# Input projection and attention of the first block merged into one loop of 32 steps, the adaptive sums moved into two down projections

## What is computed

```
proj = h @ w_in                      # q (16 heads x 64), k and v of 3 branches (4 groups x 64), gates
k_cmp, v_cmp, k_sel, v_sel, k_win, v_win = ...
kc = gelu(blocks(k_cmp + pos) @ w1[0]) @ w2[0]      # 31 blocks of 32 tokens, stride 16
vc = gelu(blocks(v_cmp + pos) @ w1[1]) @ w2[1]
o_cmp = softmax(q . kc, masked) @ vc                # 31 keys
o_sel = softmax(q . k_sel, causal) @ v_sel          # up to 512 keys
o_win = softmax(q . k_win, causal) @ v_win          # up to 512 keys
o = gate0 * o_cmp + gate1 * o_sel + gate2 * o_win
return o @ w_out
```

## Time and profile before

| | us |
|---|---|
| median of 3 runs | 2434.73 (2434.29 to 2435.03) |
| the profiled execution's own time | 2437.86 |
| its span | 2436.1 |
| TensorE busy | 2296.4 (94%) |
| DVE / ACT / POOL busy | 1389.7 / 822.6 / 254.3 |
| first matmul | 10.55 |
| last matmul of NSA_IN begins | 131.96 |
| first score of the attention | 160.49 |
| first matmul of NSA_OUT | 481.29 |

### The profile page before, as it was taken

The page is one execution under the profiler, slowest core; times in us unless marked ns, Lnnn a source line. Parts: engine busy times, 40 slices in busy tenths (PEclk is TensorE's granted clock), DMA queues, the critical chain, the costliest instruction groups (busy, mean ns, idle before and its releaser), DMA issues.

```text
span 2436.1 us, 28016 instructions
## 1 busy us (share of the span) xinstructions
PE 2296.4 (94%) x10752; PEld 1847.9 (76%) x10752; DVE 1389.7 (57%) x2557; ACT 822.6 (34%) x1459; POOL 254.3 (10%) x199
## 2 busy tenths in 40 slices
PE   8988989989999998999868989999999998999997
PEld 6866667777888886888757868888877887888886
DVE  4367788657777336864777458776334645333323
ACT  4223344435443224443323334443222223222221
POOL 0035454320000002000241020000000000000000
PEclk9977889999999998999888999999988997999998
DMA  4442222123332331333000313333322221333331
GB/s 164 132 141 73 83 79 79 40 61 95 95 95 91 91 96 56 109 95 92 22 1 1 95 52 113 91 92 90 94 75 78 93 91 35 108 89 95 89 94 59
DMA packets 58804, 202.59 MB, mean 83 GB/s; under 512 B 6704, under 2 KB 6704, under 8 KB 58288
## 3 DMA queue, kind: packets, MB, share of 16 engines
q1 hardware_dynamic: 55920, 191.36, 25.9%
q10 hardware_dynamic: 2752, 9.44, 1.1%
HBM read 197.63 MB, written 2.10 MB: 82 GB/s over the span
## 4 chain that ended last, share of the span: by engine, by line
PE 87%; DVE 6%; issue 3%; POOL 2%; ACT 2%; DMA 0%; POOLq 0%; DVEq 0%; SPq 0%; ACTq 0%
PE bank L545 23%; PE bank L546 23%; PE bank L547 23%; PE bank L678 3%; PE bank L648 2%; PE bank L503 2%; PE bank L663 2%; PE bank L649 1%; POOL h L442 1%; PE bank L681 1%; PE bank L617 1%; PE bank L772 1%; PE bank L530 1%; DVE ssum L1232 1%; PE bank L806 1%
## 5 line engine op out<-in xcount | busy, mean ns | idle before, releaser
L545 PE MATMUL bank<-xhi,whi 128*128 128x512 f32 x1776 | 710.8, 400 | 28.0 <-DVE xlo L1212 22.6
L546 PE MATMUL bank<-xlo,whi 128*128 128x512 f32 x1776 | 708.4, 399 | 0.0
L547 PE MATMUL bank<-xhi,wlo 128*128 128x512 f32 x1776 | 707.8, 399 | 0.0
L1200 DVE TENSOR_TENSOR wlo<-raw,whi 128x1024 fp32r<-128x1024 f32 (+1 forms) x322 | 387.6, 1204 | 423.6 <-ACT whi L891 423.6
L891 ACT ACTIVATE whi<-raw 128x1024 fp32r<-128x1024 f32 (+1 forms) x322 | 334.8, 1041 | 808.1 <-PE bank L547 794.0
L545 PEld LDWEIGHTS bank<-xhi,whi 128*128 128x128 f32 x1776 | 337.5, 190 | 112.1 <-DVE xlo L1212 12.8
L547 PEld LDWEIGHTS bank<-xhi,wlo 128*128 128x128 f32 x1776 | 337.3, 190 | 82.5
L546 PEld LDWEIGHTS bank<-xlo,whi 128*128 128x128 f32 x1776 | 337.6, 190 | 81.8
L545 PE MATMUL bank<-hid_hi,whi 128*128 128x512 f32 x528 | 208.9, 396 | 0.0
L546 PE MATMUL bank<-hid_lo,whi 128*128 128x512 f32 x528 | 208.6, 395 | 0.0
L547 PE MATMUL bank<-hid_hi,wlo 128*128 128x512 f32 x528 | 208.6, 395 | 0.0
(11 more groups left out here) (265 smaller groups left out, 2756.8 us busy)
## 6 DMA issues: line engine op xcount, KB each, us to landing
raw<-w SPq DMA_DIRECT2D x298, 512.0 KB, 3.6
ada_w<-w_ada SPq DMA_DIRECT2D x64, 384.0 KB, 3.1
raw<-w SPq DMA_DIRECT2D x24, 384.0 KB, 3.1
h<-xT ACTq DMA_DIRECT2D x8, 256.0 KB, 9.3
w1st<-w_cmp ACTq DMA_DIRECT2D x1, 2048.0 KB, 14.3
w_v<-w_cmp ACTq DMA_DIRECT2D x1, 2048.0 KB, 8.3
out_t<-h ACTq DMA_DIRECT2D x8, 256.0 KB, 2.0
swp<-qkv ACTq DMA_DIRECT2D x2, 512.0 KB, 6.0
```

The costliest lines, as they stand in the source:

```text
L545: pe.matmul(bk, whi[w][:, cols], hi[:, k, :], start=first, stop=False)
L546: pe.matmul(bk, whi[w][:, cols], lo[:, k, :], start=False, stop=False)
L547: return pe.matmul(bk, wlo[w][:, cols], hi[:, k, :], start=False, stop=last)
L1200: dve.tensor_tensor(wlo[g % SLOTS][:, 0:n], raw[g % RAWS][:, 0:n], whi[g % SLOTS][:, 0:n].bitcast(F32), ALU.subtract).then_inc(s_lo, 1)
```

## The change

1. NSA_IN is put in another order: compressed k, compressed v, the four value panels, the gates, the first key panels, then q. Panels 13 to 20 are no longer multiplied ahead of the attention: they stand inside its loop as `filler`, two blocks (6 matmuls) a step, and panels 13 and 14 whole in two steps ahead of it.
2. Compression reads 33 columns per group with a stride of 16 out of a doubled copy (`dk`, `dv`: half of the partitions shifted by one token, made by four DMAs each, L1186). The position term is the 33rd column and comes in as the gelu's bias. `swp` and `flatten` are gone. `w1` is loaded at the start.
3. The attention has 32 steps s = (tile t, query panel qt), qt in the order 3, 2, 0, 1. A step holds four units (two branches r, two halves a). The compressed branch runs once per tile for all four query panels (`compressed_scores`, `compressed_masked`, `compressed_exps`, `compressed_scaled`, `turn_compressed`). All copies of transposed probabilities are ACT's. In `scores` and `pv` the two halves a alternate from one matmul to the next.
4. The first 6 of 8 blocks of the first three NSA_OUT panels stand in the last two steps (`out_ahead`).
5. The adaptive sums go out of the attention: 32 blocks into DOWN1 and 32 into DOWN2 (ring of 3, two accumulators). Their loads stand in SP's list two behind each of 16 weight panels; `spread_ada` stands ahead of tiles 3, 5, 6 and 7.

In the diff the three loops over i are those of TensorE, ACT and DVE, in this order; behind them stand the loads in SP's list and the line in `gemm`.

```diff
+STEPS = 32
+QT_ORDER = (3, 2, 0, 1)
...
+FILLER = {-2: [(13, kb) for kb in range(8)], -1: [(14, kb) for kb in range(8)]}
+for _m in range(6):
+    for _r in range(4):
+        FILLER[4 * _m + _r] = [(15 + _m, 2 * _r), (15 + _m, 2 * _r + 1)]
...
+            def compress_in(kv):
...
+                        mm = pe.matmul(bank[kv][:, hh * 132:(hh + 1) * 132], w1[:, m, hh * P:(hh + 1) * P],
+                                       dup[:, :, 2 * m:2 * m + 16 * 32 + 1:16], start=m == 0, stop=m == 15)
...
+            def scores(s):
...
+                for r in range(2):
+                    for a in range(2):
+                        rows, g = slice(a * HD, (a + 1) * HD), 2 * r + a
+                        if s:
+                            pe.wait_ge(s_sc, 4 * (s - 1) + g + 1)
+                        pe.matmul(bank[g][:, 0:n], qb[rows, t, qt * P:(qt + 1) * P], kb_[rows, r, j, 0:n],
+                                  start=True, stop=True).then_inc(s_S, 1)
...
+            def pv(s):
...
                 for r in range(2):
                     for kb in range(qt + 1):
+                        for a in range(2):
+                            g = 2 * j + a
+                            pe.matmul(out_slice(qt)[a * HD:(a + 1) * HD, :],
+                                      vtok[:, kb, r * 256 + g * HD:r * 256 + (g + 1) * HD],
+                                      pt[:, s % 2, 2 * r + a, kb * P:(kb + 1) * P], start=r == 0 and kb == 0,
+                                      stop=False, skip_group_check=True)
...
+            for i in range(-2, STEPS + 1):
...
+                if i + 2 < STEPS:
+                    scores(i + 2)
+                units = turned_units(i) if 0 <= i < STEPS else []
+                for u in range((len(units) + 1) // 2):
+                    turn(i, u)
+                filler(i)
+                if i >= STEPS - 1:
+                    for kb in range(3):
+                        out_ahead(3 * (i - STEPS + 1) + kb)
+                for u in range((len(units) + 1) // 2, len(units)):
+                    turn(i, u)
+                if units and i % 4 == 0:
+                    turn_compressed(i // 4)
+                if i >= 0 and after_step(i) is not None:
+                    compressed_scores(after_step(i))
+                if i >= 1:
+                    pv(i - 1)
...
+            for i in range(-2, STEPS + 2):
+                if i - 1 in PANEL_ENDS:
+                    weight_hi(PANEL_ENDS[i - 1] + SLOTS)
...
+                if i >= 2:
+                    out_hi(i - 2)
+                if 0 <= i < STEPS:
+                    keep_turned(i)
+                if i + 2 < STEPS:
+                    exps(i + 2)
+                if i >= 0 and after_step(i) is not None:
+                    compressed_exps(after_step(i))
...
+            for i in range(-2, STEPS + 2):
+                if i - 1 in PANEL_ENDS:
+                    nsa_take(PANEL_ENDS[i - 1], 7)
...
+                if i >= -1 and i + 1 < STEPS:
+                    scaled(i + 1)
+                if i >= 2:
+                    out_low(i - 2)
+                if i + 2 < STEPS:
+                    masked(i + 2)
+                if i >= 0 and after_step(i) is not None:
+                    compressed_masked(after_step(i))
...
+                if i - 1 in PANEL_ENDS:
+                    weight_lo(PANEL_ENDS[i - 1] + SLOTS)
+                if i % 4 == 2 and (i + 2) // 4 < 8:
+                    compressed_scaled((i + 2) // 4)
...
+                for half, name in enumerate(("DOWN1", "DOWN2")):
+                    k = g - START[name] - 7
+                    if 0 <= k < 16:
+                        sp.wait_ge(s_pe, START[name])
+                        for n in (2 * k, 2 * k + 1):
+                            load_ada(KD * ADA_HALF * half + n)
...
+                    if ada is not None and t in ADA_TILES:
+                        spread_ada(ada + ADA_TILES.index(t))
```

More of the change, by code:

```diff
@@ L556, in gemm @@
                     for kb in range(nb):
+                        if off + kb < skip or (only is not None and off + kb >= only):
+                            continue
                         pe.wait_ge(s_xt, XT[name] + off + kb + 1)
@@ L565, in gemm @@
                                 mm.then_inc(s_pe, 1)
+                if only is not None:
+                    return
                 if q is not None:
@@ new lines, in _ @@
+            whole(K_FIRST, 3)
+            pe.wait_ge(s_gelu, 2)
+            pe.wait_ge(s_v, 1)
+            for g in range(4):
+                for hh in range(2):
+                    mm = pe.matmul(bank[4][(g % 2) * HD:(g % 2 + 1) * HD, (g // 2) * NC:(g // 2 + 1) * NC],
+                                   w2[0][:, hh, :], hg[:, hh, g, 0:NC], start=hh == 0, stop=hh == 1)
+            mm.then_inc(s_cm, 1)
+            pe.wait_ge(s_ev, taken(GATES))
+            whole(K_FIRST + 1, 2)
+            pe.wait_ge(s_gelu, 4)
@@ new lines, in compressed_scores @@
+            def compressed_scores(t):
+                pe.wait_ge(s_ev, taken(Q_PANEL[t]))
+                for a in range(2):
+                    turn_bank_free(pe, SCORE_AT[t] + a)
+                for qt in range(NT):
+                    for a in range(2):
+                        rows = slice(a * HD, (a + 1) * HD)
+                        mm = pe.matmul(turn_bank(SCORE_AT[t] + a)[:, 32 * qt:32 * qt + NC],
+                                       qb[rows, t, qt * P:(qt + 1) * P], kct[rows, t // 4, :], start=True, stop=True)
+                mm.then_inc(s_cs, 1)
@@ L684, in spread_ada @@
-            def spread_ada(t):
-                pe.wait_ge(s_ada_k, KD + KD * t)
-                for f in range(ADA_SLICE // P):
-                    mm = pe.matmul(bank[2][:, 256 + f:257 + f], ada_acc[:, f * P:(f + 1) * P], ones[:, 0:1],
-                                   start=True, stop=True)
-                mm.then_inc(s_adap, 1)
-            def tile(t, j, jp):
-                for k in range(8 if j is not None else 4):
-                    for stage, lag in ((scores, 0), (pv, 4), (turn, 2)):
-                        at_ = unit(k, lag, t, j, jp)
-                        if at_:
-                            stage(*at_)
@@ new lines, in pv, with filler @@
+                for a in range(2):
+                    mm = pe.matmul(out_slice(qt)[a * HD:(a + 1) * HD, :], vz[:, qt, 2 * j + a, :],
+                                   ptc[:, t % 2, a, :], start=False, stop=True, skip_group_check=True)
+                mm.then_inc(s_pv, 1)
+            def filler(i):
+                for c, kb in FILLER.get(i, ()):
+                    if kb == 0:
+                        pe.wait_ge(s_lo, c + 1)
+                        pe.wait_ge(s_ev, taken(c - 1))
+                    mm = product(psum_ap(7), c, kb, kb, kb == KD - 1, xhi, xlo)
+                    if kb == KD - 1:
+                        mm.then_inc(s_pe, 1)
```

745 lines of the change are left out of this document (425 added, 320 removed).

## The result

| | us |
|---|---|
| before, median of 4 runs | 2434.88 (2434.29 to 2436.27) |
| changed kernel, median of 4 runs | 2326.11 (2324.71 to 2331.31) |
| ratio | 0.9543, 95% interval 0.9515 to 0.9572 |
| profiled execution of the changed kernel; its span | 2324.71; 2323.0 |

The change saves 108.8 us. The forecast was 2304 us, 22 less than measured and inside its range.

A forecast was written before the change was run, and what follows sets the result against it. Stages were taken as bounded by TensorE, the new attention loop by the DVE and ACT chain. -151.4 us through the attention and +20.6 in DOWN1 and DOWN2 give -130.8 on 2434.7: 2304 us, range 2272 to 2350.

The forecast's parts named there:

- Ahead of the loop: Before the attention loop: eight panels moved out, compression products 7.9 us each, no stride cost; loop begins at 105.5 us.
- Chain of DVE and ACT: Attention loop: serial chain masked, exps, scaled, out_low sets the pace, 26.4 us a tile, 209 us for eight.
- TensorE's halves: Attention loop: alternating halves cut pv from 9.4 to 5.2 us, scores 9.5 to 4.8; TensorE 22 to 23 a tile.
- Rival (a): Attention loop: scores don't pair, TensorE becomes the bound at about 29.7 us a tile; 2330 us; chance 0.17.
- The whole loop: Attention loop with lead-in and tail: 16.4 + 209 + 4 = 229 us, with 8 for clock 237, end at 342.5.
- The 8 us for the clock: Attention loop: loss to a lowered TensorE clock, 8 us taken, between 0 and 20.
- Adaptive sums: DOWN1 and DOWN2: four spreads 5.3 us plus 5 us wait for the last slice, 10.3 a stage, +20.6 for both.
- rival (b): DOWN1 and DOWN2: POOL loses DVE's whole instruction, slice 29.4 us, 12 us more per stage; 2328 us; chance 0.16.
- Rival (d): Attention loop: half clock throughout, +173 us, 2477 us, slower than before; chance 0.02.
- Rival (e): Prologue: something such as compression weights on DMA queues holds the first panels, up to 15 us, 2319; chance 0.08.

The follow-up runs named there:

- b1: Changed kernel with key and value features stored by residue of the token modulo 16, so compression products read without a stride: 2314.29 us, ratio 0.9463.
- c2: Changed kernel with VectorE's loop order masked (step i+2), out_low (step i-2), scaled (step i+1): 2313.09 us.
- d3: Changed kernel with all four score products of a step reading rows 0 to 63, the first half: 2343.22 us.
- the rerun: The changed kernel itself run once more, unaltered, on another chip: 2327.43 us, ratio 0.9544 to the kernel before.
- b2: Changed kernel with the loads of the adaptive weights two panels earlier in SyncE's queue: 2309.56 us, ratio 0.9459.
- e1: Changed kernel with three repairs together (features by residue, adaptive loads two panels earlier, VectorE's order masked, out_low, scaled): 2279.23 us, ratio 0.9348.

## Why the prediction was right, and where it was off

Right in direction and in mechanism; 22 us too low. The profiled execution went from 2437.86 to 2324.71, -113.2 where the sum had -130.8. By its terms:

1. **Ahead of the loop: the term that failed.** The prediction wrote of the stride of 16 that it had no row, gave "between nothing and a doubling", and took nothing, "since the columns are as wide in bytes as before". It was the doubling: 2 x (14.62 - 7.9) = 13.4 us. The width of a column is not the point; the distance between elements is, 8 bytes being nearly free and 16 not. The loop began 16.0 us late, and b1, without the stride, 1.6 us late: taking nothing for a term that was itself bounded at 15.8 us is what made most of the miss.
2. **Chain of DVE and ACT: right.** 26.4 us a tile forecast, 26.46 measured; DVE's idle time ahead of the reciprocal was 1.98, 1.11 and 1.79 us, forecast 1 to 2. c2 shows that it was this order that bound. It also shows only 1 us of distance to the next bound, less than the forecast "22 to 23 us" of TensorE suggested: it is 24.10 us, and its waits come on top.
3. **TensorE's halves: right.** The 32 instructions of `pv` at query panel 3 were forecast at 2.1 us and took 1.80 (2.12 with the compressed part); scores at 1.8 and took 1.92. Rival (a), scores that don't pair, was given 29.7 us a tile; d3 made them so and got 28.9. The whole loop was forecast at 237 us. From its start to the end of the block it kept to that: the start came 16.0 us late and the block's end 15.8 (135.6 us saved where 151.4 were forecast). The 8 us for the clock were about right: c2's loop, all at 1.00, gained 14 us on this profile and 12 on the rerun's, 8 of them by its shorter tiles.
4. **Adaptive sums: the wait right, its price too small.** Forecast were four spreads of 5.3 us and a wait of 4 to 5 us ahead of tile 7 alone, 10.3 us a stage. The spreads are 5.3 (b2), the waits 5.23 and 5.45 and only there, but the stages grew by 14.0 and 14.9. The half clock behind the wait was not in the sum: 3.5 us or more each. POOL's slice was forecast at 26.2 us, and in POOL's timeline the slices take 25.2 to 27.0 us; they are ready 39, 65, 92 and 117 us into DOWN1, forecast 37, 63, 90 and 116. So POOL lost only part of DVE's time, as taken, and rival (b), by which a slice takes 29.4, is out. What neither the sum nor rival (b) had is that DVE loses too: its weight remainders (L1413) take 1.225 us in the median of the whole kernel and 1.80 while POOL has its slices in DOWN1. The Trainium skill (SBUF — State Buffer, Who interferes with whom) has the lock last for the whole instruction; the measured spacing is under what the prediction worked out from that.
5. **The SSD stage, not in the sum.** It was 476.9 us before and 471.7 in the changed kernel. But the rerun of the same kernel has 477.2, at a granted clock of 0.92 in the stage where the first profile has 0.94. The other runs, all with the same SSD stage, lie between 473.4 (e1) and 477.1 us (b2). So these 5 us are not to be put down to the change; what decides the clock there stays open.

Rival (d), a half clock through the loop, did not come: by c2 the dips cost some 4 to 6 us. Rival (e) did not come either: no wait for transfers stood ahead of the loop. The gain that was missed lies in the terms above: +15.8 up to the end of the attention block, +8.3 in the down projections, -5.2 in the SSD stage and -1.3 in all the rest, together 17.6. The 5.2 are luck: without them the forecast would have been some 23 us too low on this profile. The remaining 4.4 us are the medians: the profiled execution of before lay 3.0 us over its median, that of the changed kernel 1.4 under.

## What to carry to other kernels

When a change gives a matmul a strided moving operand, look at the distance between its elements before counting columns (fp32 doubled in price from 16 bytes on), and let the producer write them in the order of reading. Price a wait in a dense TensorE stage with the half clock behind it, here 3.5 us on 5.2, and look at where a producer starts in the loading queue before making it faster. When an engine in a chain is moved, ask which buffer its last instruction frees: two orders of the same instructions gave +6.6 us and -14 us, by the place of one of 0.28 us.

## What was not expected of the hardware

- fp32 moving operand, 132 columns: the product takes 7.37 us at stride 1, 7.99 at 2 and 15.29 at 4, with 15.52 and 14.62 at 8 and 16: not monotone beyond the step.
- Score products of two row halves overlap though two products of one half stand next to each other (1.92 and 1.93 us for four in the two orders, 3.63 on one half). In `pv` two products of one column half in a row keep the overlap too (0.81 us in both orders); four in a row lose most of it (1.73 against 1.24).
- After a wait of 5.23 us in a dense stage TensorE ran 6.6 us at 0.50, the 12 one-column instructions and nine dense matmuls.
- With two-input DVE instructions and POOL both at work on SBUF, both get longer: DVE's weight remainder 1.80 us in place of 1.225, POOL's slice 25.2 to 27.0 us in place of the 20.8 that its instructions take alone.
